# Post norm sums between the output tiles, and the first output tiles of a stage computed together by contraction index

## The chip, the cores and the metric

The kernel runs on one core of one Trainium2 chip. The metric is the device time of one execution in microseconds; the median of several runs is given. The engines work side by side, each through its own queue in order, and wait for each other on semaphores: PE (TensorE, matrix products), ACT (ScalarE, activations), DVE (VectorE), POOL (GpSimd) and SP (SyncE, which here issues the DMAs).

## The reference

Two transformer blocks on one sequence of 256 tokens of width 1024, all in float32. The first block puts 16 meta tokens in front (272 tokens), the second works on the 256.

```python
# first block
f = swiglu(rmsnorm(h, ffn1_pre_g), w_gate, w_up, w_down)      # inner width 2816
h = h + 0.5 * rmsnorm(f, ffn1_post_g)
m = hybrid_mixer(rmsnorm(h, mix_pre_g), ...)                   # two attentions, gates, out projection
h = h + rmsnorm(m, mix_post_g)
f = swiglu(rmsnorm(h, ffn2_pre_g), ...)
h = h + 0.5 * rmsnorm(f, ffn2_post_g)
# second block
h = rms_norm(x, norm1_g) * (1.0 + sc1) + sh1                   # n1
z = h @ w_in                                                   # conv values and gates, q, k, v, gates
x = x + g1 * (mixed @ w_out)
x = x + g2 * moe_ffn(rms_norm(x, norm2_g) * (1.0 + sc2) + sh2, ...)   # 32 experts, 4 of them a token
return rms_norm(x, final_g)
```

A pre norm feeds the stage that follows it, a post norm is applied to a stage's output before it is added to the residual.

## The kernel before

Activations lie transposed: 8 tiles of 128 features (`KD = 8`), each 272 or 256 tokens wide. A weight matrix comes as a stream of pieces, each 128 x 2048 (16 blocks of 128 x 128, 1 MB), into a ring of six slots (`ring`, L497). SP loads a piece when PE has begun one that lies five further back: PE reports this on the semaphore `freed` (L496).

Accuracy in float32 is kept by splitting: a weight piece is copied by ACT into `w_hi` in a rounded format (L1168, in `split_piece`), and the rest `w - w_hi` is written into `w_lo` by DVE (L1536, in `rest`) or, for the second block, by POOL in four slices (L1491). There are three split buffers, and ACT may fill one only when PE has begun the piece behind the one that used it last (`freed` again, L1167). Inputs are split in the same way into `x_hi` (ACT, L1174) and `x_lo` (DVE, L1572). One block product is then three matmuls, `w_hi x_hi`, `w_hi x_lo`, `w_lo x_hi` (`three`, L575 to L577), added up in a PSUM bank.

A norm needs the sum of squares over all 1024 features. ACT squares the tiles into `sq`, PE multiplies them by a matrix of ones and adds them up in bank 7 (`norm_sum`, L565 to L571: eight matmuls, each run as two passes), ACT makes the inverse root from it (`root`, L1153: Ln at L1158, Exp at L1159, behind the load of their function table if another is in), and DVE applies it (L1516). For a post norm DVE also adds the result to the residual `res` (`residual`, L1552), ACT squares that (L1151) and PE sums it for the following pre norm.

An FFN runs 22 up tiles j (`up_tile`, L584): for each, two outputs g (gate and up) over 8 indices k, 48 matmuls, into banks `2*(j%2)+g`. Tile j waits for its split weights (`w_lower`) and for the hidden values of tile j - 2 (`hid_ready`), which have left the same banks: Silu on ACT (L1189), multiply on DVE (L1600), then the two parts of the hidden value. Between them DVE computes one row block of the adaLN modulation a tile (L1588). For the first tile PE waits for each `x_split` in turn. Then 8 output tiles m follow, each over 22 blocks (L608 to L622); ACT squares and copies them (L1202, L1203). In the first mixer's last projection (L879) it is L1357 and L1358. After the eighth tile `norm_sum` runs for the post norm (L695, L883, L886).

Mix 1 begins with seven tiles `lat` (L699), two alternating banks, evacuated by ACT (L1234), then eight tiles q and k; the second block's first stage (n1) with four pairs `conv` (L892), four alternating banks, whose gate half goes through a sigmoid on ACT (L1383) and is multiplied on DVE (L1757). Both wait for the inputs of the first tile one by one (`split_x_first`, L687) and go through all k of a tile before the next tile. The order of all this is written out by hand; nothing reorders it.

Of the kernel before, what the change touches and what calls it, by code (L numbers as in the profile page):

```python
# [26 lines left out]
P = 128  # L27
D = 1024
KD = D // P
SEQ = 256  # L30
# [145 lines left out]
def build(nc, xT_in, stream, ada, c_in, cols_in, const_in, w_exp_in, w_exp_out, b_exp, out):  # L176
# [6 lines left out]
    with ctx:  # L183
# [377 lines left out]
        def _(pe):  # L561
# [3 lines left out]
            def norm_sum(n, tiles, width, squares=sq):  # L565
# [5 lines left out]
                last.then_inc(n_sum, 1)  # L571

            def three(out_, wh, wl, xh, xl, start, stop):

                begin = mm(out_, wh, xh, start=start, stop=False)  # L575
                mm(out_, wh, xl, start=False, stop=False)  # L576
                return begin, mm(out_, wl, xh, start=False, stop=stop)  # L577

            def ffn(f, at, lo):
# [3 lines left out]

                def up_tile(j, piece, hid_at, first=False):  # L584

                    pe.wait_ge(w_lower, piece)
                    pe.wait_ge(hid_ready, hid_at)
                    for g in range(2):
                        for k in range(KD):
                            c0 = (g * KD + k) * P  # L590
                            b = j % SPLIT_BUFS
                            if first and g == 0:
                                pe.wait_ge(x_split, AT[x_split]["f1_pre" if f == 0 else "f2_pre"] + k + 1)
                            begin, last = three(bank[2 * (j % 2) + g][:, 0:w], w_hi[:, b, c0:c0 + P],
                                                w_lo[:, b, c0:c0 + P], x_hi[:, k, lo:TOK], x_lo[:, k, lo:TOK],
                                                k == 0, k == KD - 1)
                            if g == 0 and k == 0:
                                begin.then_inc(freed, 1)
                    last.then_inc(up_ready, 1)

                ahead = NF % RING
                for j in range(ahead):
                    up_tile(j, ORDER[at] + j + 1, base + j + 1, first=(j == 0))
                with pe.Fori(0, NF // RING) as it:
# [3 lines left out]
                for m in range(KD):  # L608
                    pe.wait_ge(down_out, f * KD + m + 1)
                    for k in range(NF):  # L610
# [10 lines left out]
                        at_block += 1  # L621
                    last.then_inc(down_ready, 1)  # L622

            class Cursor:
# [42 lines left out]
            def natural(cur, n_k, parts, ready):  # L667
# [13 lines left out]
                last.then_inc(ready, 1)  # L681

            def split_x(k, lo, hi):

                return x_hi[:, k, lo:hi], x_lo[:, k, lo:hi]
# [8 lines left out]
            ffn(0, FFN1_AT, 0)  # L694
            norm_sum("f1_post", KD, TOK)  # L695
            norm_sum("mix_pre", KD, TOK)
            pe.wait_ge(const_rest, 16)
            cur = Cursor(MIX1_AT)
            for i in range(7):  # L699
                if i >= 2:  # L700
                    pe.wait_ge(evac["lat"], i - 1)
                tile(cur, bank[i % 2][:, 0:TOK], lambda k: split_x_first("mix_pre", k, 0, TOK) if i == 0
                     else split_x(k, 0, TOK), KD, proj)
            for i in range(8):
# [174 lines left out]
            for m in range(KD):  # L879
                if m >= 2:  # L880
                    pe.wait_ge(evac["w1"], m - 1)
                tile(cur, bank[4 + m % 2][:, 0:SEQ], lambda k: nrm[:, k, 0:SEQ], KD, proj)
            norm_sum("mix_post", KD, SEQ)  # L883
            norm_sum("f2_pre", KD, SEQ)
            ffn(1, FFN2_AT, META)
            norm_sum("f2_post", KD, SEQ)  # L886

# [3 lines left out]
            x2 = lambda k: split_x(k, 0, SEQ)  # L891
            for m in range(CT):  # L892
                if m >= 2:
                    pe.wait_ge(evac["conv"], m - 1)
                tile(cur, bank[2 * (m % 2)][:, 0:SEQ], x2 if m else lambda k: split_x_first("n1", k, 0, SEQ), KD)
                tile(cur, bank[2 * (m % 2) + 1][:, 0:SEQ], x2, KD, proj)
# [227 lines left out]
        def _(act):  # L1124
# [106 lines left out]
            for i in range(7):  # L1231
                two_ahead(i, MIX1_AT, MIX1_AT + MIX1_PROJ - 1)
                act.wait_ge(proj, AT[proj]["lat"] + i + 1)
                A(lat[:, i, :], bank[i % 2][:, 0:TOK], ACT.Copy).then_inc(evac["lat"], 1)  # L1234
            act.wait_ge(evac["lat"], 5)
# [851 lines left out]
```

## Time and profile before

| | us |
|---|---|
| median of 3 runs | 1991.53 (1990.17 to 1993.28) |
| profiled execution | 1990.33, span 1988.5 |
| PE busy | 1903.7 (96%) |
| first FFN, mix 1, FFN 2, n1 and the dense rest | up to about 980 |
| expert loop | from about 990 to 1975 |

Times in the rows are in us from the start of the span. PE is the matmul side of TensorE, PEld its weight loads. A row in order of time gives start, length, engine, line, operation, output<-inputs and, in brackets, how long the engine was idle before and what ended that. Matmuls overlap, so their lengths add up to more than the time that they take; the distance between the starts of two is what one costs. The granted clock is a share of 2.4 GHz: 1.00 or 0.50 (1.2 GHz) at any moment, something between for a stretch that has both.

### The profile page before, as it was taken

Reading aid. Unit: us, or ns where it says so; the run is one execution under the profiler, and the core shown is the slowest. Engines: PE = TensorE matmul, PEld = TensorE weight load, DVE = VectorE, ACT = ScalarE, POOL = GpSimd, SP = SyncE. Lnnn points to the kernel's source line nnn. Section 1 sums busy time; section 2 is a strip of 40 time slices with the busy share of each in tenths; the row PEclk is TensorE's granted clock in tenths of the full one; section 3 lists DMA queues with packets and bytes.
Section 4 is the critical chain, followed back from the end, with each engine's and each line's share of the span. In section 5 each row is a group of like instructions: output and inputs, shape, how many; then the busy total and the mean of one; then the engine's idle time right before and its main releaser. Section 6 shows DMA issues by size and latency. Waiting matters only on the chain.

```text
span 1988.5 us, 28458 instructions
## 1 busy us (share of the span) xinstructions
PE 1903.7 (96%) x10964; PEld 1165.5 (59%) x10965; DVE 826.9 (42%) x1497; ACT 506.4 (25%) x831; POOL 141.2 (7%) x108
## 2 busy tenths in 40 slices
PE   7999898999899989997899999999999999999997
PEld 7999886678799978776633333333333333333333
DVE  6776532352577436997322322222222221221223
ACT  5333434531533454235201100110110110110111
POOL 0000000000000028446100000000000000000000
PEclk9999998999999999888799999999999999999999
DMA  9777341124385534223689999999999999999793
GB/s 346 257 260 266 138 170 64 64 86 159 128 285 211 182 116 161 94 85 106 220 335 416 420 417 417 419 417 417 419 417 418 419 417 418 419 417 418 293 419 138
DMA packets 98796, 560.10 MB, mean 282 GB/s; under 512 B 8977, under 2 KB 11153, under 8 KB 50449
## 3 DMA queue, kind: packets, MB, share of 16 engines
q1 hardware_dynamic: 98544, 558.82, 71.7%
q8 instruction: 41, 0.67, 0.1%
q10 hardware_dynamic: 192, 0.46, 0.1%
q14 instruction: 19, 0.15, 0.0%
HBM read 558.20 MB, written 1.05 MB: 281 GB/s over the span
## 4 chain that ended last, share of the span: by engine, by line
PE 80%; DVE 9%; DMA 6%; ACT 3%; issue 1%; POOL 0%; DVEq 0%; SPq 0%; ACTq 0%
PE bank L1045 20%; PE bank L1110 10%; PE bank L575 9%; PE bank L577 9%; PE bank L576 9%; DVE arena L1516 6%; DMA ring<-w_exp_in 5%; PE bank L659 3%; PE bank L1056 3%; PE bank L1029 3%; PE bank L1076 3%; PE bank L569 2%; PE bank L1101 2%; PE bank L1035 1%; ACT arena L1471 1%
## 5 line engine op out<-in xcount | busy, mean ns | idle before, releaser
L1045 PE MATMUL bank<-ring,arena 128*64 128x512 f32 x2112 | 471.7, 598 | 1.9 <-DMA ring<-w_exp_in 1.9
L575 PE MATMUL bank<-x_hi,w_hi 128*128 128x256 f32 (+1 forms) x1272 | 374.9, 295 | 18.0 <-DVE x_lo L1572 11.3
L577 PE MATMUL bank<-x_hi,w_lo 128*128 128x256 f32 (+1 forms) x1272 | 368.2, 290 | 0.0
L576 PE MATMUL bank<-x_lo,w_hi 128*128 128x256 f32 (+1 forms) x1272 | 368.2, 289 | 0.0
L1045 PEld LDWEIGHTS bank<-ring,arena 128*64 128x64 f32 x2112 | 145.9, 137 | 308.2 <-issue 297.9
L575 PEld LDWEIGHTS bank<-x_hi,w_hi 128*128 128x128 f32 x1272 | 247.5, 195 | 34.1 <-issue 25.2
L577 PEld LDWEIGHTS bank<-x_hi,w_lo 128*128 128x128 f32 x1272 | 248.1, 195 | 0.0
L576 PEld LDWEIGHTS bank<-x_lo,w_hi 128*128 128x128 f32 x1272 | 247.7, 195 | 0.0
L1536 DVE TENSOR_TENSOR w_lo<-ring,w_hi 128x2048 fp32r<-128x2048 f32 x84 | 192.3, 2290 | 128.9 <-ACT w_hi L1168 128.9
L1110 PE MATMUL bank<-ring,arena 128*64 128x512 f32 x1056 | 233.9, 595 | 0.0
L1168 ACT ACTIVATE w_hi<-ring 128x2048 fp32r<-128x2048 f32 x110 | 210.0, 1909 | 63.8 <-PE bank L575 63.4
L1491 POOL TENSOR_TENSOR w_lo<-ring,w_hi 128x512 fp32r<-128x512 f32 x104 | 141.0, 1390 | 810.7 <-ACT w_hi L1168 810.7
L1926 DVE TENSOR_SCALAR arena<-cst 32x64 f32<-32x64 f32 x66 | 15.8, 239 | 425.3 <-PE bank L1056 425.3
L1468 ACT ACTIVATE arena<-arena 128x512 f32<-128x512 f32 x33 | 20.8, 631 | 574.4 <-DVE arena L1520 574.4
L1110 PEld LDWEIGHTS bank<-ring,arena 128*64 128x64 f32 x1056 | 72.9, 137 | 158.7 <-issue 158.7
L577 PE MATMUL bank<-hid_hi,w_lo 128*128 128x272 f32 (+1 forms) x352 | 100.0, 284 | 0.0
L575 PE MATMUL bank<-hid_hi,w_hi 128*128 128x272 f32 (+1 forms) x352 | 100.0, 284 | 0.0
L576 PE MATMUL bank<-hid_lo,w_hi 128*128 128x272 f32 (+1 forms) x352 | 99.7, 283 | 0.0
L1516 DVE SCALAR_TENSOR_TENSOR arena<-arena,col 128x256 f32<-128x256 f32 x120 | 97.6, 813 | 4.0
L1520 DVE TENSOR_SCALAR arena<-bank 128x512 f32<-128x512 f32 (+1 forms) x34 | 23.0, 677 | 183.0 <-PE bank L1045 182.9
L1933 DVE TENSOR_TENSOR arena<-arena,bank 128x512 f32<-128x512 f32 x136 | 86.1, 669 | 9.2 <-PE bank L1056 9.2
L1478 ACT ACTIVATE arena<-bank 128x512 f32<-128x512 f32 x33 | 19.7, 597 | 249.7 <-PE bank L1110 249.7
(279 smaller groups left out, 1965.1 us busy)
## 6 DMA issues: line engine op xcount, KB each, us to landing
ring<-w_exp_in SPq DMA_DIRECT2D x256, 1024.0 KB, 17.0
ring<-w_exp_out SPq DMA_DIRECT2D x128, 1024.0 KB, 16.4
ring<-stream SPq DMA_DIRECT2D x120, 1024.0 KB, 4.8
arena<-ada SPq DMA_DIRECT2D x48, 512.0 KB, 3.8
cst<-const_in SPq DMA_DIRECT2D x1, 1568.0 KB, 19.4
res<-xT_in SPq DMA_DIRECT2D x1, 1088.0 KB, 5.9
arena<-c_in SPq DMA_DIRECT2D x2, 512.0 KB, 8.5
outT<-arena SPq DMA_DIRECT2D x2, 512.0 KB, 3.0
```

Of the source, the lines that this page charges most:

```text
L575: begin = mm(out_, wh, xh, start=start, stop=False)
L576: mm(out_, wh, xl, start=False, stop=False)
L577: return begin, mm(out_, wl, xh, start=False, stop=stop)
L659: begin = last = mm(out_, w, x, start=flags[0], stop=flags[1])
L1029: last = mm(to[pr, :], S[:, t, :], h2n[:, t, 512 * j:512 * j + 512], start=(t == 0), stop=(t == 1), tile_position=pos)
L1045: last = mm(bank[2 + gu][pr, :], xT[:, k % 4, k // 4, :], ring[:, k, c0:c0 + 512], start=False, stop=(k == KD - 1), tile_position=pos)
L1110: last = mm(bank[5][pr, :], hmT[:, k % 4, k // 4, :], ring[:, s, c0:c0 + 512], start=False, stop=(k == KD - 1), tile_position=pos)
L1168: A(w_hi[:, BUF[p], :], ring[:, p % RING, :], ACT.Copy).then_inc(w_high, 1)
L1491: nc.gpsimd.tensor_tensor(w_lo[:, BUF[p], c:c + REST_COLS], ring[:, p % RING, c:c + REST_COLS], w_hi[:, BUF[p], c:c + REST_COLS].bitcast(f32),
L1516: return V.scalar_tensor_tensor(out=out_, in0=in0, scalar=scalar, in1=in1, op0=op0, op1=op1)
L1536: tt(w_lo[:, BUF[p], :], ring[:, p % RING, :], w_hi[:, BUF[p], :].bitcast(f32), ALU.subtract)\
L1933: last = tt(a_, a_, bank[banks[j]][:, :].rearrange("p (a b) -> p a b", a=2), ALU.add)
```

## The change

1. `sum_tile` adds one square tile into bank 7 where the sums of the whole norm stood before. For the three post norms (after FFN 1, the first mixer, FFN 2) the sum of tile m - 1 is issued behind output tile m, and only the last one behind all. The three `norm_sum` calls go.
2. The first output tiles of a stage run together, k outside and tiles inside: in FFN 1 the two outputs of j = 0 (`begun = 1`), in FFN 2 those of j = 0 and 1 (`begun = 2`), in mix 1 the first four `lat` tiles, now in banks 0 to 3, in n1 the first two conv pairs. All their weights are waited for ahead. The first piece is reported on `freed` at the first matmul, the second only at the last k, and the tiles' ends are reported one behind the other at the last k.

Arithmetic and instruction counts stay the same.

```diff
--- before.py
+++ after.py
@@ -570,6 +570,14 @@
                               start=(m == 0), stop=(m == tiles - 1))
                 last.then_inc(n_sum, 1)
 
+            def sum_tile(n, m, tiles, width, squares=sq):
+
+                pe.wait_ge(n_sq, AT[n_sq][n] + m + 1)
+                last = mm(bank[7][:, 0:width], const("ones"), squares[:, m, 0:width],
+                          start=(m == 0), stop=(m == tiles - 1))
+                if m == tiles - 1:
+                    last.then_inc(n_sum, 1)
+
             def three(out_, wh, wl, xh, xl, start, stop):
 
                 begin = mm(out_, wh, xh, start=start, stop=False)
@@ -581,7 +589,27 @@
                 w = TOK - lo
                 base = f * NF
 
-                def up_tile(j, piece, hid_at, first=False):
+                def first_tiles(js):
+
+                    for j in js:
+                        pe.wait_ge(w_lower, ORDER[at] + j + 1)
+                        pe.wait_ge(hid_ready, base + j + 1)
+                    for k in range(KD):
+                        pe.wait_ge(x_split, AT[x_split]["f1_pre" if f == 0 else "f2_pre"] + k + 1)
+                        for j in js:
+                            for g in range(2):
+                                c0 = (g * KD + k) * P
+                                begin, last = three(bank[2 * j + g][:, 0:w], w_hi[:, j, c0:c0 + P],
+                                                    w_lo[:, j, c0:c0 + P], x_hi[:, k, lo:TOK], x_lo[:, k, lo:TOK],
+                                                    k == 0, k == KD - 1)
+                                if k == 0 and j == 0 and g == 0:
+                                    begin.then_inc(freed, 1)
+                                if k == KD - 1 and g == 0 and j:
+                                    begin.then_inc(freed, 1)
+                            if k == KD - 1:
+                                last.then_inc(up_ready, 1)
+
+                def up_tile(j, piece, hid_at):
 
                     pe.wait_ge(w_lower, piece)
                     pe.wait_ge(hid_ready, hid_at)
@@ -589,8 +617,6 @@
                         for k in range(KD):
                             c0 = (g * KD + k) * P
                             b = j % SPLIT_BUFS
-                            if first and g == 0:
-                                pe.wait_ge(x_split, AT[x_split]["f1_pre" if f == 0 else "f2_pre"] + k + 1)
                             begin, last = three(bank[2 * (j % 2) + g][:, 0:w], w_hi[:, b, c0:c0 + P],
                                                 w_lo[:, b, c0:c0 + P], x_hi[:, k, lo:TOK], x_lo[:, k, lo:TOK],
                                                 k == 0, k == KD - 1)
@@ -599,8 +625,10 @@
                     last.then_inc(up_ready, 1)
 
                 ahead = NF % RING
-                for j in range(ahead):
-                    up_tile(j, ORDER[at] + j + 1, base + j + 1, first=(j == 0))
+                begun = 1 if f == 0 else 2
+                first_tiles(range(begun))
+                for j in range(begun, ahead):
+                    up_tile(j, ORDER[at] + j + 1, base + j + 1)
                 with pe.Fori(0, NF // RING) as it:
                     for j in range(ahead, ahead + RING):
                         up_tile(j, it * RING + (ORDER[at] + j + 1), it * RING + (base + j + 1))
@@ -620,6 +648,9 @@
                             begin.then_inc(freed, 1)
                         at_block += 1
                     last.then_inc(down_ready, 1)
+                    if m:
+                        sum_tile("f1_post" if f == 0 else "f2_post", m - 1, KD, w)
+                sum_tile("f1_post" if f == 0 else "f2_post", KD - 1, KD, w)
 
             class Cursor:
 
@@ -680,6 +711,23 @@
                             cur.owed = 0
                 last.then_inc(ready, 1)
 
+            def four_tiles(cur, outs, n, lo, hi, signals, lower_sem, order, per):
+
+                p = cur.b // BLK
+                for q in (p, p + 1):
+                    pe.wait_ge(lower_sem, (order[q] + 1) * per)
+                for k in range(KD):
+                    x = split_x_first(n, k, lo, hi)
+                    for i, out_ in enumerate(outs):
+                        c = (i % 2 * KD + k) * P
+                        b = BUF[p + i // 2]
+                        begin, last = three(out_, w_hi[:, b, c:c + P], w_lo[:, b, c:c + P], *x, k == 0, k == KD - 1)
+                        if (k, i) in ((0, 0), (KD - 1, 2)):
+                            begin.then_inc(freed, 1)
+                        if k == KD - 1 and i in signals:
+                            last.then_inc(proj, 1)
+                cur.b += 4 * KD
+
             def split_x(k, lo, hi):
 
                 return x_hi[:, k, lo:hi], x_lo[:, k, lo:hi]
@@ -692,15 +740,13 @@
 
             norm_sum("f1_pre", KD, TOK)
             ffn(0, FFN1_AT, 0)
-            norm_sum("f1_post", KD, TOK)
             norm_sum("mix_pre", KD, TOK)
             pe.wait_ge(const_rest, 16)
             cur = Cursor(MIX1_AT)
-            for i in range(7):
-                if i >= 2:
-                    pe.wait_ge(evac["lat"], i - 1)
-                tile(cur, bank[i % 2][:, 0:TOK], lambda k: split_x_first("mix_pre", k, 0, TOK) if i == 0
-                     else split_x(k, 0, TOK), KD, proj)
+            four_tiles(cur, [bank[i][:, 0:TOK] for i in range(4)], "mix_pre", 0, TOK, range(4), w_lower, ORDER, 1)
+            for i in range(4, 7):
+                pe.wait_ge(evac["lat"], (i - 3) if i < 6 else 5)
+                tile(cur, bank[i % 2][:, 0:TOK], lambda k: split_x(k, 0, TOK), KD, proj)
             for i in range(8):
                 if i >= 2:
                     pe.wait_ge(evac["qk"], i - 1)
@@ -880,19 +926,20 @@
                 if m >= 2:
                     pe.wait_ge(evac["w1"], m - 1)
                 tile(cur, bank[4 + m % 2][:, 0:SEQ], lambda k: nrm[:, k, 0:SEQ], KD, proj)
-            norm_sum("mix_post", KD, SEQ)
+                if m:
+                    sum_tile("mix_post", m - 1, KD, SEQ)
+            sum_tile("mix_post", KD - 1, KD, SEQ)
             norm_sum("f2_pre", KD, SEQ)
             ffn(1, FFN2_AT, META)
-            norm_sum("f2_post", KD, SEQ)
 
 
             norm_sum("n1", KD, SEQ)
             cur = Cursor(MIX2_AT)
             x2 = lambda k: split_x(k, 0, SEQ)
-            for m in range(CT):
-                if m >= 2:
-                    pe.wait_ge(evac["conv"], m - 1)
-                tile(cur, bank[2 * (m % 2)][:, 0:SEQ], x2 if m else lambda k: split_x_first("n1", k, 0, SEQ), KD)
+            four_tiles(cur, [bank[i][:, 0:SEQ] for i in range(4)], "n1", 0, SEQ, (1, 3), w_split, POOL_ORDER, RESTS)
+            for m in range(2, CT):
+                pe.wait_ge(evac["conv"], m - 1)
+                tile(cur, bank[2 * (m % 2)][:, 0:SEQ], x2, KD)
                 tile(cur, bank[2 * (m % 2) + 1][:, 0:SEQ], x2, KD, proj)
             pe.wait_ge(x_whole, KD)
             for k in range(KD):
@@ -1231,7 +1278,7 @@
             for i in range(7):
                 two_ahead(i, MIX1_AT, MIX1_AT + MIX1_PROJ - 1)
                 act.wait_ge(proj, AT[proj]["lat"] + i + 1)
-                A(lat[:, i, :], bank[i % 2][:, 0:TOK], ACT.Copy).then_inc(evac["lat"], 1)
+                A(lat[:, i, :], bank[i if i < 4 else i % 2][:, 0:TOK], ACT.Copy).then_inc(evac["lat"], 1)
             act.wait_ge(evac["lat"], 5)
             for i in range(8):
                 two_ahead(7 + i, MIX1_AT, MIX1_AT + MIX1_PROJ - 1)
```

## Rows read from the trace of the kernel before

**Rows 1.** Busy time of each engine over the whole span (page, part 1)
```profile
PE 1903.7 (96%) x10964; PEld 1165.5 (59%) x10965; DVE 826.9 (42%) x1497; ACT 506.4 (25%) x831; POOL 141.2 (7%) x108
```

**Rows 2.** Busy by stretch: length; PE, PEld, DVE, ACT, POOL busy (count); PE clock; DMA
```profile
152.00:218.30 66.30, 66.30 (x532) 66.30 (x531) 40.04 (x38) 25.94 (x26) 0.00 (x0) 1.00 0.70 256
...
483.00:510.60 27.60, 27.60 (x128) 24.32 (x129) 4.58 (x2) 8.20 (x16) 0.00 (x0) 1.00 0.46 163
```

**Rows 3.** Order of time, end of the first FFN: start, length, instruction [idle before]
```profile
218.38 3.83 PE L569 MATMUL bank<-sq,cst 128*128 128x272 f32 x16
218.57 0.40 ACT L1202 ACTIVATE sq<-bank 128x272 f32<-128x272 f32 x1 [3.92 <-PE bank L577]
...
219.28 1.28 ACT L1142 ACT_TABLE_LOAD   x1
222.24 0.49 ACT L1158 ACTIVATE rtmp<-bank,cst 128x272 f32<-128x272 f32 x1 [1.68 <-PE bank L569]
```

**Rows 4.** One norm-sum matmul (L569), min/median/max in ns
```profile
L569 PE MATMUL bank<-sq,cst x136: 379/392/796, 7.2 to 1980.4; 128*128 128x256 f32 x88, 128*128 128x272 f32 x48
```

**Rows 5.** Order of time, end of the first mixer (post norm)
```profile
510.71 3.62 PE L569 MATMUL bank<-sq,cst 128*128 128x256 f32 x16
...
511.59 1.28 ACT L1142 ACT_TABLE_LOAD   x1
514.37 0.47 ACT L1158 ACTIVATE rtmp<-bank,cst 128x256 f32<-128x256 f32 x1 [1.50 <-PE bank L569]
```

**Rows 6.** Order of time, end of the second FFN (post norm)
```profile
715.31 3.62 PE L569 MATMUL bank<-sq,cst 128*128 128x256 f32 x16
...
718.97 0.47 ACT L1158 ACTIVATE rtmp<-bank,cst 128x256 f32<-128x256 f32 x1 [1.50 <-PE bank L569]
```

**Rows 7.** Order of time, PE and its weight loads, first tiles of mix 1
```profile
233.45 0.36 PE L575 MATMUL bank<-x_hi,w_hi 128*128 128x272 f32 x1 [2.67 <-DVE x_lo L1572]
...
236.59 0.33 PEld L576 LDWEIGHTS bank<-x_lo,w_hi 128*128 128x128 f32 x1
...
236.82 0.33 PEld L577 LDWEIGHTS bank<-x_hi,w_lo 128*128 128x128 f32 x1
...
237.35 0.33 PEld L576 LDWEIGHTS bank<-x_lo,w_hi 128*128 128x128 f32 x1
...
248.13 0.29 PE L577 MATMUL bank<-x_hi,w_lo 128*128 128x272 f32 x1
```

**Rows 8.** PE by stretch: length, busy (count), granted clock, DMA; mix 1 and FFN 2
```profile
234.80:235.60 0.80, 0.66 (x3) 0.87 0.98 154
...
238.80:239.60 0.80, 0.80 (x8) 0.99 0.00 0
...
525.20:526.00 0.80, 0.33 (x1) 0.71 0.00 0
...
528.40:529.20 0.80, 0.80 (x5) 0.66 1.06 451
```

**Rows 9.** Order of time, first and 96th split matmul of FFN 2
```profile
525.67 0.55 PE L575 MATMUL bank<-x_hi,w_hi 128*128 128x256 f32 x1 [2.60 <-DVE x_lo L1572]
...
539.35 0.28 PE L577 MATMUL bank<-x_hi,w_lo 128*128 128x256 f32 x1
```

**Rows 10.** Order of time, ACT and DVE after FFN 2's second up tile
```profile
539.67 0.38 ACT L1189 ACTIVATE arena<-bank 128x256 f32<-128x256 f32 x1 [3.41 <-PE bank L577]
...
540.98 0.41 DVE L1600 TENSOR_TENSOR arena<-arena,bank 128x256 f32<-128x256 f32 x1
```

**Rows 11.** Order of time, POOL and PE in the second block's first stage
```profile
741.71 19.93 POOL L1491 TENSOR_TENSOR w_lo<-ring,w_hi 128x512 fp32r<-128x512 f32 x16 [24.69 <-ACT w_hi L1168]
...
746.86 0.36 PE L575 MATMUL bank<-x_hi,w_hi 128*128 128x256 f32 x1 [1.97 <-POOL w_lo L1491]
```

**Rows 12.** Order of time, start of the second up tile of FFN 1
```profile
22.73 2.29 DVE L1536 TENSOR_TENSOR w_lo<-ring,w_hi 128x2048 fp32r<-128x2048 f32 x1 [1.36 <-ACT w_hi L1168]
...
25.07 0.39 PE L575 MATMUL bank<-x_hi,w_hi 128*128 128x272 f32 x1
```

## The prediction

> **What bounds the kernel now.** I read the page's busy times first: PE is busy for 1903.7 of the span of 1988.5 us [rows 1], so work that is added to PE's queue is paid unless it falls into one of its few gaps. Then the busy time by stretch. In the down stage of the first FFN PE is busy for the whole 66.30, and so it is in the two other stages that end in a post norm, 27.60 of 27.60 and 65.30 of 65.30 [rows 2]: no slack there. DMA is busy for 0.46 to 0.70 of them, so weights are not what is waited for. The same rows give the price of one split matmul at the high clock level: 66.30 / 532 = 0.125 us with 272 columns, 65.30 / 556 = 0.117 with 256. (A matmul's own row says 0.28, because they overlap; spacing is what counts.) Last I read the boundaries in order of time, where PE does wait: for the post norm [rows 3 to 6], for the next stage's inputs [rows 7 to 10], and for POOL [rows 11].
>
> **Part 1: the post norm sums move between the tiles.** Nothing is added or dropped: eight sums of two matmul passes each, three times. In the old place 16 passes take 3.83; less the last one's own 0.39 [rows 4] over 15 spacings that is 0.229, or 0.46 a sum with 272 columns, and (3.62 - 0.39) / 15 x 2 = 0.43 with 256 [rows 3, 5, 6].
>
> What is added: after the change sums 0 to 5 run before the last tile. That tile ends 6 x 0.46 = 2.75 later in the first FFN, 6 x 0.43 = 2.58 later in each of the other two stages: 7.9 us, all on PE in stretches without a gap [rows 2]. The wait for the squares costs nothing: ACT squares a tile 0.2 after it ends (218.57 against 218.38 [rows 3]) and the sum for it is queued a whole tile later.
>
> What is removed: the run from the end of the last tile to the square root's first instruction (L1158) is now 222.24 - 218.38 = 3.86, 514.37 - 510.71 = 3.66 and 718.97 - 715.31 = 3.66. After the change only sums 6 and 7 are left. The last square ends 0.59 after the tile, its sum is through by about 1.1, and with 0.2 to the reader PE would be done at 1.3. But ACT has a table load there first, which ends 219.28 + 1.28 = 220.56, that is 2.18 after the tile (2.16 in the second case [rows 5]; I take 2.16 for the third). It hid behind the sums; now it is what is late. So each run shrinks to 2.17, not to 1.3: 1.69 + 1.49 + 1.49 = 4.7 saved.
>
> Part 1 is thus +7.9 - 4.7 = **+3.2 us**. The price of a sum in mid-stream is not shown: from below it is the same two passes (PE runs in order and has no gap, which excludes less); from above I allow 0.05 a sum for its wait, the step from a DVE result at 25.02 to PE at 25.07 [rows 12], 21 x 0.05 = 1.1 more. I take none of it, since PE's queue is full there.
>
> **Part 2: the first tiles of a stage, index by index.** The inputs of a stage come 0.76 apart (236.59 to 237.35, the same operand of two successive k), and one tile has only three matmuls for each, 0.37 at the high level [rows 7]. Four tiles have 1.5, so PE is never short of input. What can be won is the time PE has now over its pure work, up to the end of the fourth output tile, and only if what follows is ready.
>
> Mix 1: 96 matmuls run from 233.45 to 248.13, 14.8 with the last one's spacing [rows 7]. Pure work is 96 x 0.125 = 12.0. But the clock falls to 0.50 within 234.8 to 235.6 and is back at 238.8 [rows 8], some 3.3 us, in which the spacing is 0.23 (236.59 to 236.82). Before, PE would have waited for inputs anyway and lost little by it; four tiles lose 3.3 x (1 - 0.125 / 0.23) = 1.5. The group takes 13.5: **-1.3** (bounds 0 and -2.8, the latter with the clock high throughout).
>
> FFN 2: 96 matmuls (two outputs for each of two j) from 525.67 to 539.35, 13.8 [rows 9]; pure work 11.3; the clock is low from the first one on (0.71 over the slice that begins before it [rows 8]), again 1.5: 12.8, so -1.0. Against it stands a new wait: tile 2 takes over the banks of tile 0, whose end now comes just six matmuls before the end of the group. Silu starts 0.32 after the last matmul of a tile, takes 0.38, the multiply 0.41 [rows 10], and 0.05 to PE [rows 12]: 1.16, of which seven spacings, 0.82, are covered. +0.3 exposed; net **-0.7** (bounds 0 and -2.2).
>
> The second piece is also reported free only near the end of the group. Queued behind that on ACT is its split of piece 3, on DVE the rest of that split (2.29 [rows 12]) after the hidden values of tile 0 and an adaLN row. With ACT's part taken as no longer than DVE's (an estimate) the piece is whole some 4.6 to 5 after the group, and PE wants it a tile of 5.7 later: covered, with under 1 us to spare; without that cover it costs its excess, once. SP's load of a later piece waits for the same report, but it is five pieces ahead. In mix 1 the same delay has two tiles of 3.0 as cover.
>
> FFN 1: j = 0 alone, so the change only mixes its two outputs. Tile 1 starts at 25.07 because DVE finishes its weights at 25.02 [rows 12]; nothing upstream of that depends on PE: **0**.
>
> Second block's first stage (n1): PE ends its fourth tile and then sits idle for 1.97, until POOL has split the third piece: four slices from 741.71 on, PE at 746.86 [rows 11]. ACT's half of that split stands behind its input work, table load included, none of which waits for the tiles. What the group wins ahead of it only lengthens that idle: **0** (bounds 0 and +1.5, the latter if the longer idle adds a low stretch of the clock).
>
> **Sum.** +3.2 - 1.3 - 0.7 = **+1.2 us**. The profiled execution took 1990.3 (span 1988.5 and 1.8 around it), so it becomes 1991.5; the median of the runs, 1991.53, stands 1.2 above it, and 1991.5 + 1.2 = 1992.7, from unrounded terms (1.24) **1992.8**.
>
> **The rivals.**
> - *The clock stays high in the groups* (22%). For it: before mix 1 the clock is high at the start of the group and falls only after some 2 us of thin work; dense work might keep it. Against: in FFN 2 it is low before PE has done anything. Mix 1 then gives -2.8, FFN 2 -2.2: 3.2 - 5.0 = -1.8, 1989.7.
> - *Slower: the low level lasts twice as long in the two groups that are not covered* (15%). PE is now done about 1.3 after a last tile instead of 3.7, while the pre norm's first sum comes only 1.5 to 1.7 sooner, so PE's idle there grows by some 0.8; and dense work now stands where thin work absorbed the low clock. A second 3.3 us costs 1.5 in mix 1 and in FFN 2: +4.2, 1995.7. It decides if the granted clock is still 0.50 more than 4 us after a group has begun.
> - *The sums between the tiles are free* (6%), because matmul rows overlap (0.28 against a spacing of 0.12) and a sum might slip in. Against: back to back they cost 0.43 and nothing says they cost less elsewhere. Then -4.7 - 2.0 = -6.7, 1984.8.
> - *Changing the bank with every three matmuls breaks PE's stream* (3%). Before, the bank changes once in 24 or 48 matmuls, and the spacing there is the ordinary one as far as the stretches without a gap show [rows 2]; a change in every third is not shown. If it cost enough to hold the clock low, 96 matmuls at 0.23 (0.216 for 256 columns, scaled) take 22.1 and 20.7: +7.3 in mix 1, +6.9 in FFN 2, and in n1 6.9 less the 1.97 of idle, +4.9; with part 1 +22, 2014.
> - The Trainium skill has a rule of that kind ("TensorE: Matmul & The Clock Gate", section "A second HAM failure mode: psum-queue depth-cycling"): a kernel that cycled through PSUM banks had small idles between matmul groups, and its clock swung between the levels. By that rule the change would end near 2014; by the rows, near 1992.8. The trace has no idle where a tile changes its bank, so it does not agree, but it has no change as frequent.
>
> **How the numbers follow.** The likeliest case has 54%. A run's median here scatters by about 1 us, and about 0.2%, 4 us, is what a measurement can tell from no change. The range goes from the high-clock case less that scatter, 1988.8, to just past the slower rival, 1996.4; outside are the free sums, the bank rival and the tails, under 2 in 10. Faster by over 4 us: the free sums and a sliver of the first rival, 8%. Slower by over 4 us: ten of the slower rival's fifteen, the bank rival and a tail, 14%. Within: 78%.
>
> **What would show it.** Down stages of 69.1 and 67.9 instead of 66.3 and 65.3; Ln (L1158) about 2.2 after the last tile and right behind the table load in all three post norms; the mix 1 group over in about 13.5 and the FFN 2 group in 12.8, with a PE idle of 0.3 behind the latter until DVE's multiply; a wait for POOL of more than 1.97 in n1, ended at the same distance from the stage's start; PE's start of FFN 1's tile 1 unmoved at 25.07. I am wrong if a sum in mid-stream costs less than 0.4, if the root starts at 1.3, if the spacing in the groups is above 0.125 at the high level, or if the third piece of FFN 2 comes late.

## The result and the profile after

The changed kernel takes **1997.98 us** (1996.15 to 2000.51) against 1992.35 (1990.17 to 1993.28) for the kernel before, six executions each: ratio 1.0031, with 95% confidence between 1.0018 and 1.0044. Timed a second time (below) it is 1.0028 [1.0018, 1.0039]. It is some 6 us slower, where +1.2 was forecast and 1996.4 was the upper end of the range.

The page of the changed kernel, its busy times and the granted clock in 40 slices of the span:

```profile
PE 1906.8 (96%) x10964; PEld 1171.9 (59%) x10965; DVE 826.8 (41%) x1497; ACT 507.0 (25%) x831; POOL 141.1 (7%) x108
PEclk9999899989999989888889999999999999999999
```

PE is still the bound, at the same 96% [rows 1]. It executes what it executed before and is busy 3.1 us longer, although no matmul was added: some of them take longer or overlap less.

**The post norm.** ACT of the changed kernel in order of time, behind the last output tile of the first FFN:

```profile
222.69 0.40 ACT L1249 ACTIVATE sq<-bank 128x272 f32<-128x272 f32 x1 [3.89 <-PE bank L585]
222.98 0.39 ACT L1250 ACTIVATE nrm<-bank 128x272 f32<-128x272 f32 x1
223.39 1.28 ACT L1189 ACT_TABLE_LOAD   x1
224.69 0.49 ACT L1205 ACTIVATE rtmp<-bank,cst 128x272 f32<-128x272 f32 x1
```

The tile ends at 222.49. Ln (the last row) starts 2.20 later, right behind the table load, where it started 3.86 after the tile before [rows 3]. The forecast had 2.18. In the other two post norms it is 2.17. The sums no longer set it.

**The two groups.** PE of the changed kernel in order of time: the first matmul of the mix 1 group and its last seven (of 96), then the first and the last of the FFN 2 group and the one behind it.

```profile
237.11 0.56 PE L583 MATMUL bank<-x_hi,w_hi 128*128 128x272 f32 x1 [2.67 <-DVE x_lo L1619]
...
249.88 0.28 PE L585 MATMUL bank<-x_hi,w_lo 128*128 128x272 f32 x1
250.00 0.29 PE L583 MATMUL bank<-x_hi,w_hi 128*128 128x272 f32 x1
250.12 0.28 PE L584 MATMUL bank<-x_lo,w_hi 128*128 128x272 f32 x1
250.25 0.29 PE L585 MATMUL bank<-x_hi,w_lo 128*128 128x272 f32 x1
250.37 0.28 PE L583 MATMUL bank<-x_hi,w_hi 128*128 128x272 f32 x1
250.49 0.29 PE L584 MATMUL bank<-x_lo,w_hi 128*128 128x272 f32 x1
250.62 0.28 PE L585 MATMUL bank<-x_hi,w_lo 128*128 128x272 f32 x1
...
534.89 0.35 PE L583 MATMUL bank<-x_hi,w_hi 128*128 128x256 f32 x1 [2.60 <-DVE x_lo L1619]
...
546.14 0.28 PE L585 MATMUL bank<-x_hi,w_lo 128*128 128x256 f32 x1
546.73 0.35 PE L583 MATMUL bank<-x_hi,w_hi 128*128 128x256 f32 x1 [0.31 <-DVE arena L1647]
```

The mix 1 group takes 250.62 - 237.11 + 0.125 = 13.6 (14.8 before [rows 7]; 13.5 forecast), with 3.4 us of it at the low clock level. The FFN 2 group takes 546.14 - 534.89 + 0.117 = 11.4 (13.8 before [rows 9]; 12.8 forecast with the clock low at its start, which it was not in this execution; in the two other traces of the change it was, and the group took 12.8). Tile 2 of FFN 2 waits for the multiply, as forecast: it starts 0.59 after the last matmul of the group, 0.47 more than a spacing.

**So both parts do what they were forecast to do, and what is over that is elsewhere.** To find it, every trace is divided at the same instructions. "Low" is the time in a stretch in which the granted clock is 0.50.

| stretch | before, two traces | change, three traces | difference of the means | forecast |
|---|---|---|---|---|
| start to the third Silu of FFN 1 | 37.5, 37.6 | 38.9, 37.9, 37.3 | +0.5 | 0 |
| from there to the three post norms' Ln, in all | 386.00 twice | 389.2 three times | +3.2 | +3.2 |
| Ln to the first pre norm's Ln, three times, in all | 26.2, 25.0 | 27.1, 26.2, 26.2 | +0.9 | 0 |
| mix 1, to the sixth lat copy | 23.7, 23.8 | 22.5, 22.5, 22.5 | -1.2 | -1.3 |
| **sixth lat copy to the first square of the mixer's last projection** | 232.2, 238.4 | 238.3, 238.3, 238.3 | **+3.0** | **0** |
| FFN 2, to the third Silu | 22.3, 22.3 | 20.4, 21.7, 21.8 | -1.0 | -0.7 |
| n1, to the fourth sigmoid | 32.2, 30.7 | 32.2, 32.2, 32.2 | +0.7 | 0 |
| the rest | | | -1.0 | 0 |

The three rows for which the forecast had a number other than 0 add up to +1.0, the whole table to +5.1. The largest other row is the mixer's middle: q and k tiles, both attentions and the gates, with no edit in it. But its +3.0 rests on two traces of the kernel before that differ by 6.1 themselves. These are the rows by stretch for it (length, busy time and instructions of PE, PEld, DVE, ACT and POOL, granted clock, share of the DMA engines, GB/s), of the changed kernel:

```profile
256.99:495.32 238.33, 230.20 (x1247) 177.05 (x1246) 79.86 (x163) 93.07 (x212) 0.00 (x0) 0.94 0.29 102
```

and of the kernel before, in the execution of the front part of this document:

```profile
254.51:486.74 232.23, 224.10 (x1247) 170.90 (x1246) 79.69 (x162) 92.42 (x212) 0.00 (x0) 0.97 0.30 105
```

The same 1247 matmuls, the same idle time of PE (8.13 in both), the same work on DVE and ACT; only the clock is 0.94 and not 0.97. PE spends 27.3 us of it at the low level instead of 13.7. Over the whole span the low level holds for 114.7 and 122.7 us in the two traces of the kernel before, and for 130.5, 135.2 and 132.7 in the three of the change: 14 us more by the means. Of these, 6.8 lie in the mixer's middle, 6.3 in the three pre norm stretches, where PE mostly waits and a low clock costs little (+0.9), and 1.7 in n1. In the pre norms the two kernels do not overlap, with 10.2 and 6.8 us low before and 17.1, 13.7 and 13.7 in the change; in the mixer's middle they do.

### The profile page after: what moved, and what is told of

Its sections match the earlier page's. It is cut to its first block, busy times and chain, and to the rows that moved or that the text cites. A ratio compares the mean times of both kernels' runs of the same rounds, so it can differ in the third digit from the quotient of the medians.

```text
span 1995.8 us, 28458 instructions
## 1 busy us (share of the span) xinstructions
PE 1906.8 (96%) x10964; PEld 1171.9 (59%) x10965; DVE 826.8 (41%) x1497; ACT 507.0 (25%) x831; POOL 141.1 (7%) x108
## 4 chain that ended last, share of the span: by engine, by line
PE 82%; DVE 9%; ACT 4%; DMA 4%; issue 1%; POOL 0%; DVEq 0%; ACTq 0%; SPq 0%
PE bank L1092 22%; PE bank L1157 11%; PE bank L583 9%; PE bank L585 9%; PE bank L584 9%; DVE arena L1563 6%; PE bank L690 3%; PE bank L1103 3%; PE bank L1076 3%; DMA ring<-w_exp_in 3%; PE bank L1123 3%; PE bank L1148 2%; PE bank L569 1%; PE bank L1082 1%; ACT arena L1518 1%
## 5 line engine op out<-in xcount | busy, mean ns | idle before, releaser
L583 PE MATMUL bank<-x_hi,w_hi 128*128 128x256 f32 (+1 forms) x1272 | 374.6, 294 | 20.5 <-DVE x_lo L1619 10.5
```

## The experiments

Each kernel was timed beside the kernel before on one chip, a different chip for each of the three groups below; the kernel before has a median of 1992.54, 1993.49 and 1993.44 us in them. No kernel leaves out any of the computation.

### Each part alone, and both kernels traced again

**Part 1 alone**: `sum_tile` and its three uses, and nothing of part 2.

```diff
@@ ffn, output tiles
                     last.then_inc(down_ready, 1)
+                    if m:
+                        sum_tile("f1_post" if f == 0 else "f2_post", m - 1, KD, w)
+                sum_tile("f1_post" if f == 0 else "f2_post", KD - 1, KD, w)
...
-            norm_sum("f1_post", KD, TOK)
```

> Part 1 alone: the three post norm sums between the output tiles, the first tiles of a stage as before. The trace of the change shows each down stage 1.0 to 1.1 us longer up to its Ln, three times, so +3.2 us. Theory A (the 6 us lost in the first mixer belong to the granted clock, which falls at other moments once the work is shifted): the mixer between its sixth lat tile and the first square of its last projection may take anything from 232 to 239 us here, with the low clock in it between 13 and 28 us, and the whole kernel lands between +2 and +9. Theory B (they belong to the group of four tiles in mix 1, through the later reports of its pieces): the mixer takes 232.2 as before and the kernel is +3.2 +- 0.8.

Measured: 1995.87, ratio 1.0016 [1.0007, 1.0025]: by the ratio +3.2 us, as forecast. The three stages are longer by 0.99, 1.10 and 1.10 in its trace, with 1.06, 1.09 and 1.09 forecast.

**Part 2 alone**: `first_tiles` and `four_tiles`, with `norm_sum` where it was.

```diff
             norm_sum("f1_post", KD, TOK)
...
+            four_tiles(cur, [bank[i][:, 0:TOK] for i in range(4)], "mix_pre", 0, TOK, range(4), w_lower, ORDER, 1)
```

> Part 2 alone: first tiles of a stage by contraction index, the post norm sums back behind the last tile. Sum of the parts seen in the trace of the change: +1.5 at the start of FFN 1, -1.2 in mix 1, -1.9 in FFN 2, 0 in n1, so -1.6 without the mixer. Theory A (clock): the mixer between its sixth lat tile and the first square of the last projection may take 232 to 239, so the kernel is -1.6 to +5. Theory B (group of four in mix 1): the mixer takes 238 as in the change, +6 against before, and the kernel is about +4.5.

Measured: 1990.57, ratio 0.9989 [0.9980, 0.9998]: -2.2 us, with -2.0 forecast, so Theory B's +4.5 is out. The two parts alone add up to about +1; together they cost 6. Each of these figures is good to about 2 us, so the difference of some 5 us is clear of noise, but its size is not well known.

**The change and the kernel before, once more each**, with no edit.

> The changed kernel once more, for a second trace of it. Theory A (clock, at other moments in each execution): the mixer stretch differs from the 238.3 of the first trace by a us or more and follows the time at the low clock in it, 27.4 us in the first trace. Theory B (something fixed in the change): it is again 238.3 within 0.5.

Measured: 1997.97, on the same chip as the two parts alone, the mixer's middle again 238.3. By the words of the expectation that is Theory B, something fixed in the change. The next trace speaks against it.

> The kernel before once more, for a second trace of it. Theory A (clock, at other moments in each execution): the mixer stretch differs from 232.2 by up to 6 us, with more than 13.6 us at the low clock. Theory B (fixed): 232.2 within 0.5.

Measured: 1995.21. The mixer's middle of this second trace of the kernel before:

```profile
254.67:493.03 238.36, 230.24 (x1247) 175.59 (x1246) 79.77 (x162) 92.74 (x212) 0.00 (x0) 0.94 0.30 102
```

So the kernel before has the slow mixer too, in some executions (Theory A here). The trace on which the forecast rested was a fortunate one in this stretch. Part 2 alone has it as well, in a trace of 1990.57 us, so a slow mixer by itself does not make a slow execution:

```profile
251.94:490.25 238.31, 230.18 (x1247) 177.06 (x1246) 79.86 (x163) 92.97 (x212) 0.00 (x0) 0.94 0.29 102
```

while part 1 alone lies between:

```profile
255.54:490.73 235.19, 227.06 (x1247) 174.39 (x1246) 79.64 (x162) 92.83 (x211) 0.00 (x0) 0.96 0.30 104
```

Its idle time is 8.13 once more. The stretch's length is a straight line in its time at the low level: 13.7, 20.5 and 27.3 us low give 232.2, 235.2 and 238.3, that is 226.2 + 0.44 for each us. That is about what the two spacings say for dense work (1 - 0.125 / 0.23 = 0.46).

### Timed again, and the terms of the norm taken apart

**The change, timed once more.**

> The changed kernel, timed in more executions beside the kernel before. By the medians, part 1 alone is +3.3 and part 2 alone -2.0. Theory A1 (the parts add up, and what more the first measurement showed was where the clock fell in few executions): +1.3 +- 2, ratio near 1.0007. Theory A2 (the two together leave the clock low more often than either alone): again +5 to +6, ratio near 1.003, and a granted clock of 0.965 to 0.968 in nearly all executions where before has 0.968 to 0.972.

Measured: 1999.48 (1993.36 to 2003.59, 12 executions), ratio 1.0028 [1.0018, 1.0039]. The mean granted clock of its executions is 0.9663, that of the kernel before 0.9700. In the kernel before alone, over the 29 executions of this group, the time falls by 1.3 us for each 0.001 of clock (correlation -0.90). The difference of 0.0037 is thus worth about 4.8 us; of the +6.0 between the two means 1.2 are left, which is the forecast's sum. The agreement to the tenth is luck: within the other kernels the slope is between 1.0 and 1.6 us for each 0.001, by which 0 to 2.4 would be left.

**Part 1 with the table load ahead of the output tiles**, so that it no longer stands between the last square and Ln.

```diff
                 for j in range(NF // RING * RING, NF):
                     step(j, base + j + 1)
+                use("natural_log_exp_and_others")
                 m = 0
...
             open_gates("gates", graw)
+            use("natural_log_exp_and_others")
             for m in range(KD):
```

> Part 1 alone, with ACT's table load for the root moved ahead of the squares (all three post norms; nothing else). My reading: behind a last tile the table load was what came last, so Ln comes 1.3 us after the tile instead of 2.2, 0.9 less three times, -2.6 against part 1 alone, +0.6 against before. Rival (the sum of the last square is what comes last anyway): no change against part 1 alone, +3.2.

Measured: 1994.08, ratio 1.0001 [0.9992, 1.0010], by the two ratios 3.0 us less than part 1 alone (-2.6 forecast; the three stages are 2.4 shorter in the traces). ACT in order of time, at the same place:

```profile
221.55 0.40 ACT L1214 ACTIVATE sq<-bank 128x272 f32<-128x272 f32 x1 [3.89 <-PE bank L585]
221.84 0.39 ACT L1215 ACTIVATE nrm<-bank 128x272 f32<-128x272 f32 x1
222.76 0.49 ACT L1169 ACTIVATE rtmp<-bank,cst 128x272 f32<-128x272 f32 x1 [0.53 <-PE bank L576]
```

Ln starts 1.21 after the square instead of 2.00 and waits for PE's last sum. The table load was what came last, as the forecast said. The tile ends at 221.35, so the run from it is 1.4, where 1.3 was expected.

**The squares added up on DVE**: in the kernel before, DVE adds squares 0 to 6 into one tile while PE runs the output tiles, and PE sums two tiles after the last one instead of eight. Nothing stands between the tiles.

```diff
+            def post_sum(n, nth, width):
+                pe.wait_ge(sq_add, nth * (KD - 2))
+                mm(bank[7][:, 0:width], const("ones"), sq[:, 0, 0:width], start=True, stop=False)
+                pe.wait_ge(n_sq, AT[n_sq][n] + KD)
+                mm(bank[7][:, 0:width], const("ones"), sq[:, KD - 1, 0:width], start=False, stop=True)\
+                    .then_inc(n_sum, 1)
...
+            def add_square(n, nth, m, w):
+                dve.wait_ge(n_sq, AT[n_sq][n] + m + 1)
...
+                tt(sq[:, 0, 0:w], sq[:, 0, 0:w], sq[:, m, 0:w], ALU.add).then_inc(sq_add, 1)
```

> The kernel before, but DVE adds the squares of tiles 0 to 6 up during the last stage (six additions, each behind the tile's square), and PE makes two sums instead of eight, behind the last tile. Nothing is put between the tiles on PE. My reading (what counts is PE's time for the sums, 0.43 to 0.46 each, wherever they stand): the root's Ln comes 2.2 us after the last tile instead of 3.7 to 3.9, bound by the table load, and the stage does not grow: -4.7 us. Rival (a post norm is bound by ACT and DVE behind the sums, or DVE's additions delay the weights): 0 or slower.

Measured: 1990.18, ratio 0.9978 [0.9968, 0.9989]: -4.4 us, where the forecast's saving at the boundary is 4.7. ACT in order of time:

```profile
218.81 0.40 ACT L1211 ACTIVATE sq<-bank 128x272 f32<-128x272 f32 x1 [3.92 <-PE bank L586]
...
219.51 1.28 ACT L1151 ACT_TABLE_LOAD   x1
220.81 0.49 ACT L1167 ACTIVATE rtmp<-bank,cst 128x272 f32<-128x272 f32 x1
```

Ln stands behind the table load, 2.00 after the square, as in the change; and the last tile is not later than before (180.90 after the third Silu in both). The three stages are 4.6 shorter in the trace. So the -4.7 can be had without the +7.9, which comes from where the sums stood.

**All that gained, together**: the squares on DVE, the early table load, and the groups of mix 1, FFN 2 and n1.

> As the run before (squares added on DVE), with the early table load, and of part 2 the groups of mix 1, FFN 2 and n1, while FFN 1's first tile is as before. Sum: post norms 3 x (3.7 - 1.3) = -7.3, mix 1 -1.2, FFN 2 -0.5 to -1.9, n1 0: -9 to -10.4 if the granted clock does what it does before; the rival, that the clock gives it back as in the change, is -4 or less.

Measured: **1981.52** (1980.13 to 1986.97), ratio 0.9943 [0.9930, 0.9956], -11.4 us. It beats both kernels. The parts measured alone give -4.4 - 3.0 - 2.2 = -9.6. Its trace has 102.7 us at the low level, the least of all, so some of the rest is the clock. DVE's addition of one square, and ACT behind the last tile:

```profile
212.22 0.44 DVE L1655 TENSOR_TENSOR sq<-sq 128x272 f32<-128x272 f32 x1
```

```profile
218.76 0.40 ACT L1259 ACTIVATE sq<-bank 128x272 f32<-128x272 f32 x1 [3.92 <-PE bank L594]
219.06 0.39 ACT L1260 ACTIVATE nrm<-bank 128x272 f32<-128x272 f32 x1
219.98 0.49 ACT L1214 ACTIVATE rtmp<-bank,cst 128x272 f32<-128x272 f32 x1 [0.53 <-PE bank L587]
```

A square costs DVE 0.44, on an engine that is 41% busy, instead of 0.46 on PE; and the run from the square to Ln is 1.22.

### Is it the moment at which the mixer's work arrives?

The rest of the question is why the clock is low for longer in a stretch that was not edited. Four kernels delay the q and k tiles by useless sums (ones times constants into bank 7, which nobody reads), two or four of them, in the change and in the kernel before.

```diff
                 tile(cur, bank[i % 2][:, 0:TOK], lambda k: split_x(k, 0, TOK), KD, proj)
+            for _ in range(2):
+                mm(bank[7][:, 0:SEQ], const("ones"), cst[:, 0:SEQ], start=True, stop=True)
             for i in range(8):
```

**The change with two sums more.**

> The changed kernel with two idle sums (ones times constants into bank 7, read by nobody) on PE between the lat tiles and the q and k tiles of mix 1, some 0.9 us of dense work that nothing needs. Theory A (the mixer's time follows where the granted clock falls, and that depends on when its work comes): the mixer from its sixth lat tile to the first square of the last projection does not go from 238.3 to 239.2 but to 232.2, 235.2 or 238.3, plus 0.9, with 13.6, 20.5 or 27.3 us at the low clock, and the median may fall by up to 5 us although work was added. Theory B (a fixed cost of the change in the mixer): 239.2, and the median 0.9 above the change's, near +6.9 against before.

Measured: 1995.18, ratio 1.0008 [0.9997, 1.0019]. Work of 0.86 us (two sums at 0.43, an estimate from the rows [rows 5]) makes the kernel about 4 us faster against the kernel before than the change is without it. The two intervals just touch, and the change itself was timed on other chips. The mixer's middle, the 0.86 included:

```profile
252.97:487.56 234.59, 226.46 (x1251) 173.84 (x1250) 79.78 (x163) 92.87 (x212) 0.00 (x0) 0.96 0.30 104
```

Without the pad it is 233.7, with 17.1 us low; the line gives 226.2 + 0.44 x 17.1 = 233.7. That is Theory A in kind, but not one of its three values. This execution, of 1991.8 us, was also at the high level throughout the mix 1 stretch and FFN 2's first tiles, which the change never was in both; so not all of the gain lies in the mixer.

**The change with four sums more.**

> As the run before with four idle sums, some 1.7 us. Theory A: again one of 232.2, 235.2, 238.3, plus 1.7, not the same one for both delays. Theory B: 240.0, and +7.7 against before.

Measured: 2000.03, ratio 1.0026 [1.0014, 1.0039], mean clock 0.9675. Most of the gain of the first pad is gone. On this one chip the two padded kernels differ by 3.8 us in their means (1995.2 and 1999.0, eleven executions each; +-2.8 with 95% confidence), where the longer pad is 0.9 us more work.

```profile
254.48:493.06 238.58, 230.44 (x1255) 177.74 (x1254) 79.83 (x163) 92.94 (x211) 0.00 (x0) 0.95 0.29 102
```

Without the pad of 1.7 us the mixer is 236.9 in this execution, with 23.9 us low: between the first pad's and the change's.

**The kernel before with two sums more.**

> The kernel before with the same two idle sums. Theory A: its median moves by something else than 0.9, up to +5, as the mixer takes 235 or 238.3 in more executions. Theory B, and any reading in which a delay costs what it lasts: +0.9.

Measured: 1993.88, ratio 1.0000 [0.9991, 1.0009].

```profile
254.89:492.50 237.61, 229.48 (x1251) 177.05 (x1250) 79.68 (x162) 92.94 (x211) 0.00 (x0) 0.95 0.29 102
```

This execution has a mixer of 236.8 without the pad, at 23.9 us low, where 226.2 + 0.44 x 23.9 = 236.7.

**The kernel before with four sums more.**

> The kernel before with four idle sums. Theory A: something else than +1.7, between -1 and +6. Theory B: +1.7.

Measured: 1993.17, ratio 0.9996 [0.9987, 1.0006]; 0.9 and 1.7 us of work are lost in the noise here, with intervals that reach +1.8 and +1.2 us. The mixer of this trace is 236.8 without the pad, with 23.9 us low again. On the kernel before the pads thus move nothing that can be measured, and do not decide between the theories.

## Why the prediction was wrong

**Right: the price of a sum between the tiles** (+7.9). The last tile of the first FFN ends 183.55 after the third Silu (222.49 - 38.94) where it was 180.90 (218.38 - 37.48): 2.65 for six sums, 0.44 each, against 0.46 forecast. The wait costs nothing, and the rival in which the sums are free is out.

**Right: the boundary** (-4.7). Ln starts 2.20 after the tile and behind the table load; it is the load and not the sums (the early load gives it 1.4, and the sums on DVE leave it at 2.0 from the square).

**Right: the groups.** Mix 1 gives -1.2 (-1.3 forecast). FFN 2 gives -1.0 (-0.7) as the mean of one trace with -1.9, where the clock stayed high, and two with -0.5; the new wait for the multiply is 0.5 (0.3 forecast, because the step from DVE's result to PE takes 0.15 there and not 0.05). PE has no idle between 546.73 and 575, so the third piece of FFN 2 is there in time. At the two places where nothing was to be gained, PE of the changed kernel in order of time has

```profile
25.03 0.39 PE L583 MATMUL bank<-x_hi,w_hi 128*128 128x272 f32 x1 [2.48 <-DVE w_lo L1583]
...
755.48 0.36 PE L583 MATMUL bank<-x_hi,w_hi 128*128 128x256 f32 x1 [3.43 <-POOL w_lo L1538]
```

Tile 1 of FFN 1 starts when DVE has its weights (25.07 before), and in n1 PE waits for POOL for 3.43 instead of 1.97 [rows 11], which ends at the same distance from the stage's Ln (19.02, and 19.06 before).

**Right: changing the bank breaks nothing.** In the group the bank changes with every three matmuls, from 249.88 to 250.00 and from 250.25 to 250.37, and the spacing is the 0.12 to 0.13 of a stretch without a gap [rows 2]. The rule of the Trainium skill that the forecast weighed ("TensorE: Matmul & The Clock Gate", section "A second HAM failure mode: psum-queue depth-cycling") has no case here: the trace does not agree with it at this size.

**The step that failed: the clock was priced only where the edit is.** The sum bounds the granted clock inside the groups and at the n1 wait, and takes every stretch behind them as unchanged. The slower rival had the mechanism (the low level lasts longer, 1995.7), but in mix 1 and in FFN 2. By the means of the traces it is +3.0 in the mixer's middle, +0.9 in the pre norms, +0.7 in n1 and +0.5 at the start, less 1.0 in the rest. A us at the low level costs 0.44 in the mixer's middle and in n1, and less than that in the pre norms, where PE waits (+0.9 for 6.3 more at the low level). At the start the low level holds for 3.4 us in all five traces; one trace of the change has it in dense work (38.9) and the other two do not (37.9, 37.3). Of these stretches n1 had been given a bound (0 to +1.5) and was set to nothing. The arithmetic of the edit itself came out: by their ratios both parts alone are within 0.3 us of the forecast, closer than the 2 us to which they are known, and in the traces the edited stretches give +1.0 for +1.2. The error is in the term for the clock in all other stretches, which stood at nothing and measured about +4.8.

**The second failure: one trace was taken for the kernel.** The forecast put the scatter at about 1 us from three executions. The 29 executions of the second group spread from 1990.3 to 1997.7, and two traces of the same kernel differ by 6.1 us in one stretch. A stretch that costs between 232 and 238 by chance is a term with an uncertainty of 3 us for any version that shifts the odds, and no such term stood in the range.

The corrected sum goes by means, not by one trace: +3.2 - 2.0 for the two parts, and 0.0037 of clock x 1.3 us per 0.001 = +4.8, in all +6.0. It is an account after the fact and could not have been a forecast, since the clock in it is the measured one. The same working for the other kernels, each against the kernel before in its own group:

| kernel | difference of the means | by the clock | left | forecast for the work |
|---|---|---|---|---|
| change (timed again) | +6.0 | -0.0037: +4.8 | +1.2 | +1.2 |
| part 1 alone | +2.9 | -0.0007: +0.9 | +2.0 | +3.2 |
| part 2 alone | -2.5 | +0.0013: -1.6 | -0.9 | -2.0 |
| squares on DVE | -3.9 | -0.0016: +2.1 | -6.0 | -4.7 |
| change, two sums more | +1.4 | -0.0005: +0.6 | +0.8 | +2.1 |
| change, four sums more | +5.3 | -0.0023: +2.9 | +2.4 | +2.9 |
| all that gained | -11.0 | +0.0013: -1.7 | -9.3 | -9.6 |
| part 1, early table load | +0.3 | -0.0002: +0.2 | +0.1 | +0.6 |
| before, two sums more | +0.5 | +0.0005: -0.7 | +1.2 | +0.9 |
| before, four sums more | +0.1 | +0.0005: -0.7 | +0.8 | +1.7 |

With some 1.3 us between the last two columns at worst (single clocks have three digits, and their means still scatter) the work and the clock together fit every kernel.

**What stays open.** That the clock is low for longer in the change is shown, over all its executions. That the moment at which work arrives decides this is likely: with the short pad the change stands 4 us better against the kernel before although work was added, and 0.9 us more of pad costs 3.8 (+-2.8). But both are barely clear of noise, and on the kernel before no pad had an effect. Why both parts together are low for longer than either alone is not shown. One trace of it is steady: the pre norms are low for 13.7 to 17.1 us in all five traces that have both parts, the padded ones included, and for 10.2 and 6.8 us with either part alone. In which part of the mixer an execution loses its clock also varies. These are rows by stretch from 60 to 180 us behind the sixth lat copy, first of the kernel before:

```profile
314.51:334.51 20.00, 18.28 (x58) 11.21 (x59) 7.90 (x17) 7.93 (x19) 0.00 (x0) 0.74 0.25 96
334.51:354.51 20.00, 17.98 (x108) 12.02 (x106) 5.23 (x15) 10.76 (x29) 0.00 (x0) 1.00 0.15 52
354.51:374.51 20.00, 19.50 (x120) 14.03 (x121) 7.10 (x14) 12.19 (x30) 0.00 (x0) 1.00 0.15 53
...
394.51:414.51 20.00, 20.00 (x105) 13.96 (x104) 9.74 (x25) 6.46 (x18) 0.00 (x0) 0.91 0.16 54
414.51:434.51 20.00, 20.00 (x126) 14.83 (x124) 10.75 (x23) 9.49 (x22) 0.00 (x0) 1.00 0.31 106
```

and of the changed kernel:

```profile
316.99:336.99 20.00, 17.17 (x68) 10.31 (x68) 8.39 (x19) 8.60 (x22) 0.00 (x0) 0.91 0.25 95
336.99:356.99 20.00, 19.05 (x102) 13.42 (x102) 5.91 (x13) 10.37 (x27) 0.00 (x0) 0.90 0.15 53
356.99:376.99 20.00, 19.55 (x102) 14.60 (x102) 5.92 (x13) 10.59 (x26) 0.00 (x0) 0.84 0.15 52
...
396.99:416.99 20.00, 19.77 (x87) 13.98 (x87) 8.26 (x20) 6.16 (x17) 0.00 (x0) 0.74 0.16 54
416.99:436.99 20.00, 20.00 (x107) 14.24 (x106) 8.62 (x22) 7.30 (x20) 0.00 (x0) 0.91 0.16 53
```

In this execution of the kernel before, the clock falls early (0.74) and then stays high for 40 us; in that of the changed one it falls less there (0.91) and again in each of the two later stretches. By the three rows that makes 3 to 4 us more at the low level. The other 10 are in the last two rows: 0.91 and 1.00 before, 0.74 and 0.91 after, in stretches in which PE hardly idles. PE's idle time in the whole stretch is the same in sum (8.13); when in it the clock falls is what differs.

## What to carry to other kernels

Sums that are moved from a boundary into a stream without a gap are not hidden: count what they add in the stream (here 7.9) against what they take from the boundary (4.7), and look for an idle engine that can do them instead (DVE: -4.4 us, where the move cost +3.2). At a boundary ask what comes last once the named wait is gone; here it was a table load, worth another 2.4 to 3.0 us when it was moved up. And where the time of single executions follows the granted clock, take two or three traces of the kernel before, and put the spread of every long stretch with small gaps into the range, even when the edit does not touch it.

## What the runs showed of the hardware that was not expected

- The same instructions of PE (1247 matmuls, 8.13 us idle) take 232.2 or 238.4 us in two executions of one kernel; the whole difference is the time at the low clock level, 13.7 against 27.3 us, at 0.44 us each.
- With 0.86 us of useless matmuls ahead of the mixer the changed kernel stood at 1.0008 [0.9997, 1.0019] of the kernel before, with 1.7 us at 1.0026 [1.0014, 1.0039] on the same chip, and without any at 1.0028 [1.0018, 1.0039] on another.
- In a stream without a gap an fp32 sum of two passes cost 0.44 us and no more, its wait on ACT and the change of weights included; and a change of bank with every third matmul cost nothing.
